# The second block's mixer stays on the unnormed split of x; its norm factor goes into rotation tables, value copies, and gate products

## The reference, cut to what matters

```python
h = h + 0.5 * swiglu(rmsnorm_2(h, ffn1_norm), ...)
h = h + hybrid_mixer(rmsnorm_2(h, mix_norm), ...)
h = h + 0.5 * swiglu(rmsnorm_2(h, ffn2_norm), ...)
y = rmsnorm_2(h, final_norm)

def hybrid_mixer(u, pos, k_top, w_in, w_ret_out, w_att_out, w_mix_out):
    rq, rk, rv, rg, aq, ak, av, iq, ik, iw, g_ret, g_att = jnp.split(u @ w_in, offs, axis=-1)
    rq, rk = rope(rq), rope(rk) * RET_DK ** -0.5     # 4 retention heads, 256 wide
    yr = (jax.nn.silu(rg) * retention(rq, rk, rv)) @ w_ret_out   # retention ends in a norm
    aq, ak, iq, ik = rope(aq), rope(ak), rope(iq), rope(ik)      # 8 heads, 8 indexer heads
    ya = dsa_attention(aq, ak, av, iq, ik, iw, k_top) @ w_att_out # top 128 keys a query
    merged = jax.nn.sigmoid(g_ret) * yr + jax.nn.sigmoid(g_att) * ya
    return merged @ w_mix_out
```

## Time and profile before

| | before |
|---|---|
| median of 3 runs | 2106.74 us (2106.37 to 2106.82) |
| the profiled execution's own time | 2110.16 us |
| its span in the trace | 2108.4 us |
| mean granted clock of TensorE | 0.989 of full |
| PE busy | 96% of the span |
| DVE, ACT, POOL busy | 40%, 34%, 44% |
| chain that ended last | PE 84%, DVE 11%, ACT 3% |

### The profile page before, as it was taken

One profiled execution on the slowest core, in us unless ns is written; L12 is line 12 of the kernel. 1 busy time (PEld: TensorE's weight loads), 2 busy tenths in 40 slices (PEclk: granted clock), 3 DMA queues, 4 the chain that ended last, 5 costly groups with the idle time before them and its releaser, 6 DMA issues.

```text
span 2108.4 us, 30373 instructions
## 1 busy us (share of the span) xinstructions
PE 2031.9 (96%) x11428; PEld 1719.4 (82%) x11428; DVE 845.4 (40%) x1483; ACT 715.9 (34%) x1085; POOL 931.1 (44%) x1220
## 2 busy tenths in 40 slices
PE   7899999999999999998999999999999999999998
PEld 6578777789999999687887878778786888888887
DVE  7734447552222222897442223232323372222212
ACT  4632344432222222533445223232322333223221
POOL 5332211254444565542333544444443555455563
PEclk9999999999999999999999999999999999999999
DMA  5211100022222223221111322222221223223332
GB/s 183 80 50 41 41 31 31 30 95 88 96 89 91 91 99 120 69 72 51 60 61 61 108 83 81 80 75 83 73 80 62 98 82 100 99 90 98 101 100 80
DMA packets 49753, 168.80 MB, mean 80 GB/s; under 512 B 6400, under 2 KB 8576, under 8 KB 49664
## 3 DMA queue, kind: packets, MB, share of 16 engines
q1 hardware_dynamic: 45104, 160.45, 23.1%
q10 hardware_dynamic: 4560, 7.08, 1.0%
HBM read 165.42 MB, written 2.10 MB: 79 GB/s over the span
## 4 chain that ended last, share of the span: by engine, by line
PE 84%; DVE 11%; ACT 3%; issue 2%; POOL 0%; DVEq 0%; ACTq 0%; POOLq 0%
PE slot L1917 83%; DVE ix_score L1741 1%; DVE top L1737 1%; DVE ix_score L1758 1%; DVE square L1693 1%; DVE x_lo L1711 0%; DVE square L1592 0%; DVE xt L1703 0%; DVE square L1590 0%; ACT rs L809 0%; PE slot L2051 0%; DVE xt L1595 0%; PE slot L2327 0%; DVE h L1673 0%; DVE aq L1696 0%
## 5 line engine op out<-in xcount | busy, mean ns | idle before, releaser
L2407 POOL TENSOR_TENSOR w_lo<-w_raw,w_hi 128x256 fp32r<-128x256 f32 x1216 | 930.9, 797 | 1165.1 <-ACT w_hi L772 911.2
L1917 PE MATMUL slot<-x_hi,w_hi 128*128 128x264 f32 (+1 forms) x1864 | 647.5, 347 | 14.9 <-ACT lamt L934 7.9
L1917 PE MATMUL slot<-x_hi,w_lo 128*128 128x264 f32 (+1 forms) x1864 | 632.7, 339 | 0.0
L1917 PE MATMUL slot<-x_lo,w_hi 128*128 128x264 f32 (+1 forms) x1864 | 630.7, 338 | 0.0
L1917 PEld LDWEIGHTS slot<-x_hi,w_hi 128*128 128x128 f32 x1864 | 354.0, 190 | 62.6 <-issue 8.1
L1917 PEld LDWEIGHTS slot<-x_lo,w_hi 128*128 128x128 f32 x1864 | 352.9, 189 | 39.4
L1917 PEld LDWEIGHTS slot<-x_hi,w_lo 128*128 128x128 f32 x1864 | 353.9, 190 | 37.9 <-issue 1.2
L772 ACT ACTIVATE w_hi<-w_raw 128x1024 fp32r<-128x1024 f32 x216 | 226.8, 1054 | 358.7 <-PE slot L1917 348.5
L1917 PE MATMUL slot<-f_hi,w_hi 128*128 128x264 f32 (+2 forms) x550 | 173.5, 316 | 0.0
L1917 PE MATMUL slot<-f_hi,w_lo 128*128 128x264 f32 (+2 forms) x550 | 173.3, 315 | 0.0
L1917 PE MATMUL slot<-f_lo,w_hi 128*128 128x264 f32 (+2 forms) x550 | 172.9, 314 | 0.0
(11 more groups left out here) (316 smaller groups left out, 2771.3 us busy)
## 6 DMA issues: line engine op xcount, KB each, us to landing
w_raw<-weights SPq DMA_DIRECT2D x304, 512.0 KB, 3.3
h<-x_t ACTq DMA_DIRECT2D x4, 512.0 KB, 6.0
out<-h ACTq DMA_DIRECT2D x8, 256.0 KB, 2.2
dec<-decays ACTq DMA_DIRECT2D x4, 264.0 KB, 3.5
const<-consts SPq DMA_DIRECT2D x1, 704.0 KB, 7.0
at_rot<-rotations ACTq DMA_DIRECT2D x1, 528.0 KB, 4.8
ix_rot<-rotations ACTq DMA_DIRECT2D x1, 528.0 KB, 6.6
rt_rot<-rotations ACTq DMA_DIRECT2D x1, 528.0 KB, 3.7
```

What stands on the lines that cost most here:

```text
L1917: return nc.tensor.matmul(out, lhsT, rhs, start=start, stop=stop)
L2407: nc.gpsimd.tensor_tensor(w_lo[j][:, piece], w_raw[j][:, piece], w_hi[j][:, piece].bitcast(F32), ALU.subtract).then_inc(s_lo, 1)
```

## The change

The second split is gone: all projections of the mixer read `x_hi`, `x_lo`, and what they give lacks the norm's factor. It is put in behind the products:

- The factor is kept in `rs_mix` (528 tokens on all partitions) and, by a new PSUM result `("rs_t",)` of ten small transposes on PE and a copy on DVE, in `rs_tok` with tokens on the partitions. `("rs_t",)` takes a place in the ring of slots, so the results behind it move by one slot.
- `at_rot` (rotation of `aq`, `ak`) and `rt_rot` (of `rq`, `rk`) are multiplied by it once, two DVE operations each.
- The copies of the values out of PSUM on ACT scale by `rs_tok`; a scale differs by token block, so `av` takes four copies of 128x256 for one of 128x1024, and `rv` four of 128x512 for two. The few meta and last rows (`avm`, `rvm`) are scaled by a small DVE operation each, and PE waits for `avm`'s (`s_avs`).
- Attention gates: ACT copies `ya[j]` out as it is, DVE multiplies by `rs_mix` at the steps 8, 12, 16, 20 (j = 0 to 3) or behind the last step (4 to 7), and ACT's sigmoid follows.
- Retention gates: `scaled(hd, j)` multiplies the result in its PSUM slot by `rs_mix` on DVE, and ACT's silu waits for it. Merge gates: `scaled_gate(j)` does the same ahead of the sigmoid; `scaled_gate(j + 1)` stands at the start of `merge(j)`.
- `TOP_LATE` has 5 rounds of block 3 for 11 before; six more of block 3's rounds lie ahead of the first attention step, three in `top([2, 3])` and three alone behind `admit(2)`.
- `att_hi`, `att_lo`, `relu`, `yr`, `y_hi`, `y_lo` lie in the memory that `x2` had, since `x_hi`, `x_lo` now live until the merge gates.

```diff
-TOP_LATE = {0: 2, 1: 2, 2: 2, 3: 2, 4: 2, 5: 1}
+GATE_STEPS = [8, 12, 16, 20]
+TOP_LATE = {0: 1, 1: 1, 2: 1, 3: 1, 4: 1}
...
+            def silu(hd, j):
+
+                key = ("rg", hd, j)
+                act.wait_ge(s_rgs, 4 * hd + j + 1)
+                A.sig(nc.scalar.activation(rg[:, j, :], slot(key)[:, 0:T], ACT.Silu), *evac_at(key))
...
-            m0 = made["x"]
-            for j in range(5):
-                ks = (2 * j, 2 * j + 1) if j < 4 else ()
-                V.sync()
-                for k in ks:
-                    V.sig(nc.vector.scalar_tensor_tensor(xt[(m0 + k) % 2][:], h[:, k, :], sml("mix_gain", k), rs[r % 2][:],
-                                                         ALU.mult, ALU.mult), s_xt, m0 + k + 1)
+            V.sync()
+            rotated(("ik",), ix_rot, ik[:], T, slice(64, P))
+            for i in range(2):
+                V.own(nc.vector.tensor_tensor(at_rot[:, i, :], at_rot[:, i, :], rs_mix[:], ALU.mult))
...
-                for k in ks:
-                    dve.wait_ge(s_xhi, m0 + k + 1)
-                    V.sig(nc.vector.tensor_tensor(x2_lo[:, k, :], xt[(m0 + k) % 2][:], x2_hi[:, k, :].bitcast(F32), ALU.subtract),
-                          s_xlo, m0 + k + 1)
...
             for t in range(TOP_ROUNDS - both):
                 top([2, 3] if t < early else [2])
             admit(2)
+            for _ in range(TOP_ROUNDS - both, early):
+                top([3])
...
+            def scaled(hd, j):
+
+                key = ("rg", hd, j)
+                wait_result(dve, key)
+                V.sig(nc.vector.tensor_tensor(slot(key)[:, 0:T], slot(key)[:, 0:T], rs_mix[:, TQ], ALU.mult), s_rgs, 4 * hd + j + 1)
...
+                V.own(nc.vector.tensor_scalar(rvm[0:M, :], rvm[0:M, :], rs_tok[0:M, 9:10], None, ALU.mult))
+                scaled(hd, 0)
                 dve.wait_ge(s_dec, 16 * (hd + 1))
...
+                scaled(hd, 1)
...
+                scaled(hd, 2)
                 for d in range(3):
                     wait_evac(dve, ("rg", hd, d))
...
                         src = rqk[:, d, 0:T]
+                        if d == 1:
+                            scaled(hd, 3)
                         if d == 3:
...
+            def scaled_gate(j):
+
+                key = ("gr", j)
+                wait_result(dve, key)
+                V.sig(nc.vector.tensor_tensor(slot(key)[:, 0:T], slot(key)[:, 0:T], rs_mix[:, TQ], ALU.mult), s_grs, j + 1)
+            scaled_gate(0)
+
             def merge(j):
                 def maker(dst, m):
+                    if j + 1 < KD:
+                        scaled_gate(j + 1)
                     wait_evac(dve, ("gr", j))
...
                 if j == 0:
                     few_t("iw", 2, bias[3][:, M:TT])
+                    ps = begin(("rs_t",))
+                    for c, at in enumerate([M + n * P for n in range(NQ)] + [0] + [n * P for n in range(NQ)] + [T]):
+                        w = M if c % 5 == 4 else P
+                        m = nc.tensor.transpose(ps[0:w, c * 8:c * 8 + 8], rs_mix[0:8, at:at + w], const[0:8, 0:8])
+                    m.then_inc(s_res, 1)
...
                     if e % PAIR_STEPS == 0:
                         wait_evac(pe, ("av", pair, 0))
-                        wait_evac(pe, ("av", pair, 1))
+                        pe.wait_ge(s_avs, pair + 1)
...
-                dense(("rg", hd, 0), SEQ, (x2_hi, x2_lo))
+                dense(("rg", hd, 0), SEQ)
```

More of the change, by code:

```diff
@@ L141, in results @@
             add(("iw_t",))
+            add(("rs_t",))
     for s in range(IX_STEPS):
@@ L550, in build @@
             x_lo = sb("x_lo", [P, KD, TT], F32R, scope)
[L551 to L559, removed]
         sb("x_area", [P, 2, KD * TT])
@@ L599, in build @@
             mb = lambda name, shape, dt=F32, scope=mix: sb(name, shape, dt, scope)
-            x2_hi = mb("x2_hi", [P, KD, TT], F32R)
-            x2_lo = mb("x2_lo", [P, KD, TT], F32R)
+            with ExitStack() as scope:
+                att_hi = mb("att_hi", [P, ATT_H, T], F32R, scope)
+                att_lo = mb("att_lo", [P, ATT_H, T], F32R, scope)
+            with ExitStack() as scope:
+                relu = [mb(f"relu{i}", [P, 2, T], F32, scope) for i in range(2)]
+            with ExitStack() as scope:
+                yr = mb("yr", [P, KD, T], F32, scope)
+                y_hi = mb("y_hi", [P, 4, T], F32R, scope)
+                y_lo = mb("y_lo", [P, 4, T], F32R, scope)
+            mb("mix_area", [P, 2, KD * T])
+            rs_mix = mb("rs_mix", [P, TT])
+            rs_tok = mb("rs_tok", [P, 10])
             with ExitStack() as scope:
@@ L1097, in projected @@
                 elif key == ("av", g, 0):
-                    copy_out(key, av[g % 2][:].rearrange("p a c -> p (a c)"), w=2 * T)
+                    wait_result(act, key)
+                    for n in range(NQ):
+                        ins = nc.scalar.activation(av[g % 2][:, n, :], slot(key)[:, n * 256:n * 256 + 256], ACT.Copy, scale=rs_tok[:, n:n + 1])
+                        A.own(ins) if n < NQ - 1 else A.sig(ins, *evac_at(key))
                 elif key == ("av", g, 1):
@@ L1186, in _ @@
                     made["table"] = None
-                    copy_out(("rg", hd, j), rg[:, j, :], ACT.Silu)
+                    silu(hd, j)
                 ahead(("rg", hd, 2))
@@ L1191, in _ @@
                     copy_out(("ry", hd, d), rqk[:, d, 0:T])
-                copy_out(("rg", hd, 2), rg[:, 2, :], ACT.Silu)
+                silu(hd, 2)
                 ahead(("rg", hd, 3))
@@ L1196, in _ @@
                 made["table"] = None
-                copy_out(("rg", hd, 3), rg[:, 3, :], ACT.Silu)
+                silu(hd, 3)
                 w_split(BLOCK[("rg", hd, 3)] + 1 + 3)
@@ L1818, in _ @@
                     V.sync()
-            dve.wait_ge(s_sigm, 1)
+            for j in range(4, KD):
+                wait_evac(dve, ("ga", j))
+                V.sig(nc.vector.tensor_tensor(ya[j], ya[j], rs_mix[:, TQ], ALU.mult), s_gas, j + 1)
             for j in range(KD):
+                dve.wait_ge(s_sigm, j + 1)
                 key = ("ao", j)
@@ L1825, in _ @@
             dve.wait_ge(s_rtt, 16)
+            for i in range(2):
+                V.own(nc.vector.tensor_tensor(rt_rot[:, i, :], rt_rot[:, i, :], rs_mix[:], ALU.mult))
+            def scaled(hd, j):
+                key = ("rg", hd, j)
+                wait_result(dve, key)
+                V.sig(nc.vector.tensor_tensor(slot(key)[:, 0:T], slot(key)[:, 0:T], rs_mix[:, TQ], ALU.mult), s_rgs, 4 * hd + j + 1)
             for hd in range(RET_H):
@@ L2391, in _ @@
             for j in range(KD):
-                dense(("gr", j), SEQ, (x2_hi, x2_lo))
+                dense(("gr", j), SEQ)
             for j in range(KD):
```

81 lines of the change are left out of this document (43 added, 38 removed).

## The result

The changed kernel takes 2113.72 us (median of 9 runs, 2112.49 to 2120.42) against 2106.97 for the kernel before in the same session (9 runs, 2106.37 to 2110.94). The ratio is 1.0031, with a 95% interval of 1.0023 to 1.0040: slower, by 6.7 us of medians. The forecast was 2113.5 us.

A forecast was written before the change was run, and what follows sets the result against it. PE, busy 96% of the span, was taken as the bound, so only its waits and low clock pay. Terms -1.2 + 7.1 + 0.9 = +6.8 us on the median 2106.74 gave 2113.5 us, range 2107.5 to 2118.2.

The forecast's parts named there:

- Stages 1 to 3: Indexer's projections, top-k train and first attention pair together: the changed kernel 1.2 us ahead at AS 8.
- Stage 1: Indexer's projections: the removed split ends PE's waits for ik and iq 3 and their low clock, gaining 7.0 us.
- Stage 2: Top-k: six more rounds ahead of the first attention step add 8.5 us; first softmax at 950.8, PE waiting about 10.
- Stage 3: First attention pair, AS 1 to AS 8: fewer late rounds shorten PE's softmax waits, net gain 2.7 us.
- Stage 4: Retention heads: scaled(hd, 3) delays the low parts, costing 1.7 us in heads 0 to 2, 2.0 in head 3; 7.1.
- the rival of cheap heads: Retention heads: the gate products are mostly covered, total +2.3 us, 2109.0, no measurable change; chance 0.18.
- Stage 5: Merge: eight DVE operations behind gr 7 make PE wait 0.9 us (0.3 to 2) at k = 7.
- The faster one: Top-k train: DVE's train starts earlier by its own removed work, total -4 us, 2102.7; chance 0.10.
- The one of a clock drop in each head: Retention heads: each head's wait drops the clock, total +11 us, 2117.7 or a little over; chance 0.08.

The follow-up runs named there:

- after_again: The changed kernel run once more with no edit; 2115.45 us, ratio 1.0037 to the kernel before.
- before_ring: The kernel before plus one unused small result in the ring of slots (ten transposes, a DVE copy), second split kept; 2104.11 us, ratio 0.9976.
- filler_split: The changed kernel with 16 filler operations on DVE in the places of the removed second split; 2118.95 us, ratio 1.0049 to the kernel before.
- gate3_later: The changed kernel with scaled(hd, 3) moved from ahead of the second xt to behind the third; 2110.01 us, ratio 1.0010 to the kernel before.
- merge_later: The changed kernel with scaled_gate(j + 1) moved behind the two operations of merge(j); 2114.16 us, ratio 1.0019 to the kernel before.
- old_rounds: The changed kernel with the TOP_LATE of before, 11 late rounds of block 3 for 5; 2109.04 us, ratio 1.0011 to the kernel before.
- before_rounds: The kernel before with only the changed kernel's split of rounds, 5 late and 11 ahead of the first softmax; 2113.42 us, ratio 1.0027.

## Why the prediction was right, point by point, and where it was not

**The sum.** Forecast +6.8. Medians give +6.7 and, with after_again, +8.3. The two traces give 10.2, of which 0.2 lies ahead of the fixed point, in these parts, rounded: stage A +1.4; heads 0 to 2, 1.27 each (the distance from one head to the next on PE went from 110.03 to 111.30 us) and head 3 1.9; 1.1 of lower clock behind head 3's waits, where the spell lasts 10.3 us for 3.4 before; the merge 1.9. Behind the merge the two traces are equal (379.6 us). Stages 1 to 3 were forecast to end 1.2 us ahead at AS 8 and end 1.1 behind (144.1 us from the fixed point for 143.0). The heads came out 1.4 under their term, the merge and the low clock 2.1 over theirs. So the traced executions are 3.3 us further apart than forecast, and that the medians meet the forecast to 0.1 us is in part luck: they differ by less than the traces, and why they do is left open below.

**Stage 1, head start: size right, cause half wrong.** 7.0 forecast, 6.8 measured to the first `ak`. The step said that the removed split gives it. I named the ring's move for `iq` 3 as a condition, but counted it under "the removed split". before_ring has 3.5 us of the 6.8 with the split in place (873.06 - 842.93 = 30.1 us to the first `ak`, against 33.6 before); the rest of the change, the removed split first of all, brings the other 3.3. With fillers in the split's place (filler_split) `ik`'s wait is 3.0 us and the low clock behind it is back.

**Stage 2, the train: the mechanism right, the term 1.8 short.** The forecast was 78.2 us (69.7 + 8.5), the measured length 80.0. The six rounds took what their rows said. The rest is operations of the old train that now lie beside others: a rotation's 128x512 product took 1.22 us for 0.68, the mask of block 1 0.85 for 0.42, its scaling 0.65 for 0.49, and there is a new gap of 0.46. The first softmax came at 952.9 for 950.8. A train that shifts meets other neighbours, and the rows of before don't price that. PE's wait was 8.95 and not 10, because PE itself came later, by the low clock at 912: gate3_later and merge_later, without that spell, have 9.9.

**Stage 3: right.** The gain was 2.3 for 2.7. The softmax waits were 2.6 (forecast 2.2), and the one low spell was there. That spell was forecast from three waits of before, of 1.50, 3.29 and 2.44 us, with low windows behind them. Two other waits of the same trace, of 1.67 us (at 970.41) and 2.13 (at 988.97), are followed by full clock, 1.00 from 965 until head 3, so a wait of this size alone does not fix it.

**Stage 4: right in mechanism, size 5.7 for 7.1.** `rg` 3's result was where I placed it, and the third `xt` came 1.9 later against PE (forecast 2.0). Each head lost 1.27 and not 1.7: the wait at k = 2 was 0.99 (forecast 1.2) and at k = 3 0.17 (0.4 to 0.5), since PE's first products behind a wait are slower (0.51 for 0.40 us) and use up part of the next delay. Head 3 gave 1.9 of 2.0. The last two low parts took 2.36 us together, as in before (2.38), so the rival of cheap heads fell. gate3_later shows the cause. By the Trainium skill, page "SBUF — State Buffer", section "🔬 SBUF: two separate sides", the in-place products with their source in PSUM were to stay at 0.69 whatever POOL does. The trace agrees: all 16 took 0.70, four of them beside POOL's `w_lo`. The `y_lo` operations, both inputs in SBUF, took 1.21 to 1.22 beside it (eight) and 0.68 to 0.69 without (eight). In all eight slow ones a `w_lo` of POOL had begun 0.4 to 0.5 us earlier. Six `merged_lo` of before, which began 0.1 to 0.2 us ahead of a `w_lo`, took 0.68, and the `w_lo` 1.10 to 1.17; beside the products in PSUM it took 0.72 to 0.73. So in these traces the one that starts second pays.

**Stage 5: right in mechanism, 1.9 for 0.9.** The wait was 1.2; the slower products around it make the rest. The cause is shown by merge_later.

**The rivals.** The faster one (DVE's 17.7 us count in full) failed as argued: the first `ak` waits for ACT's copy of PE's result, 1.26 us in the row above. The one of a clock drop in each head failed for heads 0 to 2: no window there is low. In head 3 it is, for 10.3 us against 3.4 before, which is 1.1 us of the total: 0.79 and 0.50 in the two windows from 1618, where the earlier trace rows had a wait too.

```profile
1618.00:1622.00 4.00, 2.11 (x6) 0.97 (x6) 1.89 (x4) 3.27 (x5) 0.00 (x0) 0.79 0.03 8
1622.00:1626.00 4.00, 1.65 (x4) 1.32 (x5) 3.40 (x4) 1.22 (x2) 3.33 (x4) 0.50 0.00 0
```

**What stays open.** Why the medians differ by less than the traces do was not settled; it may lie in which low-clock spells an execution has (below). The version with before_ring's shift and nothing else of the change has the lowest ratio of all, and whether the removed split adds to it once the rounds and gates are placed well is not resolved: 0.9976 and 0.9981 have overlapping intervals.

## What to carry to other kernels

A change that comes as one idea can hold several. Here the idea itself (one split less) brought the first `ak` about 3 us forward, and no gain in time beyond that of the ring's move is resolved; a table of rounds edited beside it cost about 6 us, and one product placed a few operations too early in each head cost 5 to 6, though three operations later it cost 0.2 a head. Test a stream's order apart from its arithmetic.

An operation that waits for a late result belongs behind everything on its engine that does not need it. And when PE waits for a rotation, look at the slot it wants before you look at the engine that rotates: one more entry in the ring took away a wait of 3.3 us, and the kernel with it was 5 us faster.

## What was unexpected of the hardware

Code that no edit touches has a spell of low clock in some executions and not in others. Window 310 to 320 of the first block, in the kernel before and in gate3_later:

```profile
310.00:320.00 10.00, 10.00 (x42) 8.92 (x39) 2.49 (x6) 1.02 (x3) 1.63 (x3) 0.52 0.17 52
```

```profile
310.00:320.00 10.00, 10.00 (x74) 9.08 (x71) 4.80 (x17) 2.49 (x8) 1.85 (x3) 1.00 0.15 52
```

PE is busy throughout in both, and does 42 matmuls in the one and 74 in the other. Of the twelve traces four have 0.51 to 0.53 there (before, after, after_again, old_rounds), two 0.87 and 0.93, six 1.00; what follows starts 6 us later in the first four (845.92 before, 839.6 in before_rounds, at the same point). The same wait of 1.8 us for `aq` near 913 is followed by a low window in the changed kernel's two traces and by none in gate3_later's and merge_later's. So a wait seen in a trace does not fix the clock behind it, and two traces must be compared by distances.
